# An interleaved two-model block on one core: new order inside the MLA and PLE stages, a stage boundary with a split moved between two adds, and 44 transposes after the second PLE

## The reference

```
ffn, even, ffn, ple, ffn, mla, ffn, ple, hybrid, ffn        then a final rms norm
ffn:    x = x + c * (silu(rms(x) @ gate) * (rms(x) @ up)) @ down       hidden width 2816
ple:    x = x + rms(sigmoid(rms(x) @ w_gate) * (p @ w_proj)) * gain
mla:    x = x + attention(8 heads, low-rank q and kv, rope) @ w_out
even:   a gated MLP over positions and a chunked recurrence; hybrid: attention, SSD and pooling
```

## Time and profile before

| | |
|---|---|
| median of 3 runs | 1418.93 us |
| the profiled execution, its own time | 1411.39 us |
| its span, first to last instruction | 1409.6 us |
| PE matmul busy | 96% of the span |
| DVE, ACT busy | 56%, 46% |
| mean granted TensorE clock | 0.981 |
| stages by time | FFN some 189 us each, even 140, MLA 108, hybrid 116, PLE 36 each |

### The profile page before, as it was taken

One profiled execution on the slowest core, in us unless ns is written; L12 is line 12 of the kernel. 1 busy time (PEld: TensorE's weight loads), 2 busy tenths in 40 slices (PEclk: granted clock), 3 DMA queues, 4 the chain that ended last, 5 costly groups with the idle time before them and its releaser, 6 DMA issues.

```text
span 1409.6 us, 17529 instructions
## 1 busy us (share of the span) xinstructions
PE 1346.7 (96%) x6634; PEld 1117.6 (79%) x6634; DVE 795.1 (56%) x860; ACT 644.2 (46%) x727; POOL 73.5 (5%) x180
## 2 busy tenths in 40 slices
PE   6999998999999999899999989999998998999997
PEld 5888888877888887688888867888886986788885
DVE  4555458635555556545446765644556796554543
ACT  5443456323544345543344754444345564543442
POOL 2000003000000000100000210000001200000000
PEclk9999999999999999899999999999999999999999
DMA  8555553413655555365554423655544451565550
GB/s 260 188 195 185 185 188 119 171 69 124 198 191 195 179 187 180 112 198 188 179 188 135 154 90 113 209 179 191 195 179 150 137 179 60 168 205 179 188 199 30
DMA packets 159116, 233.29 MB, mean 166 GB/s; under 512 B 7528, under 2 KB 126462, under 8 KB 159070
## 3 DMA queue, kind: packets, MB, share of 16 engines
q1 hardware_dynamic: 156420, 229.19, 48.8%
q10 hardware_dynamic: 2170, 2.68, 0.6%
q0 software_dynamic: 480, 0.80, 0.3%
HBM read 231.58 MB, written 1.05 MB: 165 GB/s over the span
## 4 chain that ended last, share of the span: by engine, by line
PE 86%; DVE 8%; ACT 4%; issue 1%; DMA 1%; POOL 0%; SPq 0%; ACTq 0%; POOLq 0%; DVEq 0%
PE ps L231 25%; PE ps L233 25%; PE ps L232 25%; DVE wl L203 3%; PE ps L470 2%; ACT wh L198 2%; PE ps L312 1%; PE ps L836 1%; PE ps L247 1%; DVE x_rows L412 1%; PE ps L249 1%; PE ps L248 1%; DMA raw<-in_ffn_w_up 1%; PE ps L1281 1%; ACT hth L332 1%
## 5 line engine op out<-in xcount | busy, mean ns | idle before, releaser
L231 PE MATMUL ps<-wl,hth 128*128 128x512 f32 (+2 forms) x1280 | 507.5, 396 | 18.7 <-DVE htl L345 9.4
L233 PE MATMUL ps<-wh,htl 128*128 128x512 f32 (+2 forms) x1280 | 497.9, 389 | 0.0
L232 PE MATMUL ps<-wh,hth 128*128 128x512 f32 (+2 forms) x1280 | 497.6, 389 | 0.0
L608 DVE TENSOR_TENSOR wl<-raw,wh 128x2048 fp32r<-128x2048 f32 x120 | 275.1, 2293 | 204.9 <-ACT wh L560 204.9
L231 PEld LDWEIGHTS ps<-wl,hth 128*128 128x128 f32 x1280 | 243.1, 190 | 70.9 <-issue 13.1
L203 DVE TENSOR_TENSOR wl<-raw,wh 128x2048 fp32r<-128x2048 f32 (+3 forms) x100 | 220.8, 2217 | 122.8 <-ACT wh L198 122.7
L560 ACT ACTIVATE wh<-raw 128x2048 fp32r<-128x2048 f32 x120 | 229.7, 1914 | 123.6 <-PE ps L233 123.6
L233 PEld LDWEIGHTS ps<-wh,htl 128*128 128x128 f32 x1280 | 242.6, 190 | 50.1
L232 PEld LDWEIGHTS ps<-wh,hth 128*128 128x128 f32 x1280 | 243.4, 190 | 45.9
L198 ACT ACTIVATE wh<-raw 128x2048 fp32r<-128x2048 f32 (+3 forms) x100 | 184.5, 1855 | 91.9 <-PE ps L233 70.3
L231 PE MATMUL ps<-wl,prod_h 128*128 128x512 f32 x400 | 156.1, 390 | 0.0
(11 more groups left out here) (351 smaller groups left out, 957.2 us busy)
## 6 DMA issues: line engine op xcount, KB each, us to landing
raw<-in_ffn_w_gate SPq DMA_DIRECT2D x88, 512.0 KB, 4.0
raw<-in_ffn_w_up SPq DMA_DIRECT2D x88, 512.0 KB, 4.9
raw<-in_ffn_w_down SPq DMA_DIRECT2D x88, 512.0 KB, 3.9
raw<-in_w_gate_up SPq DMA_DIRECT2D x44, 512.0 KB, 4.6
raw<-in_even_w_in SPq DMA_DIRECT2D x24, 512.0 KB, 4.6
raw<-in_w_down SPq DMA_DIRECT2D x22, 512.0 KB, 3.9
raw<-in_ple_w_gate SPq DMA_DIRECT2D x16, 512.0 KB, 3.7
raw<-in_w_in SPq DMA_DIRECT2D x16, 512.0 KB, 4.3
```

The costliest lines, as they stand in the source:

```text
L231: nc.tensor.matmul(o, xh, b, start=first, stop=False)
L232: nc.tensor.matmul(o, xh, a, start=False, stop=False)
L233: return nc.tensor.matmul(o, xl, a, start=False, stop=last)
L608: nc.vector.tensor_tensor(wl[:, r, :], raw[:, r, :], wh[:, r, :].bitcast(f32), ALU.subtract)\
```

## The change

Four parts. (1) `add_result`: only the next stage's first slot is split ahead of the adds, and the second between the halves. (2) PLE: gate slots n+1 and n+2 as before; then tile 0 with slots n+3 and n+4, then tile 1 with the same two, which stay in the ring until the end. The steps after it are done tile by tile, and `x_ready` counts four quarters. Where an FFN follows, its `x` is turned by tile and half (`turn_tile`), the first pieces stand inside the PLE's queues, and the FFN's first two slots are multiplied tile by tile. (3) Where none follows, TensorE makes 44 transposes of the identity into a free bank. (4) MLA: another order on ACT and DVE, one swap on PE, and a one-column exponential ahead.

The core of the diff:

```diff
         def add_result(dve, s, scale):
-            dve_ahead.before(dve, base[s] + SLOTS_OF[PLAN[s]] - 1)
+            following = base[s] + SLOTS_OF[PLAN[s]]
+            dve_ahead.through(dve, following)
             for half in range(2):
+                if half == 1:
+                    dve_ahead.through(dve, following + 1)
...
+            def first_by_tiles(pe):
+                turn_tile(pe, s, 0, 0)
+                turn_tile(pe, s, 0, 1)
+                for tt in range(TT):
+                    for u in range(2):
+                        take_slot(pe, n + u)
+                        turned_by(pe, s, 0, 2 * tt + u + 1)
+                        r = (n + u) % RING
+                        for kk in range(4):
+                            k, at = 4 * u + kk, kk * 2 * HC
+                            m = product(bank(tt), hth[:, k, tt * P:(tt + 1) * P], htl[:, k, tt * P:(tt + 1) * P],
+                                        wh[:, r, at:at + 2 * HC], wl[:, r, at:at + 2 * HC], k == 0, k == KT - 1)
+                            if tt == 0 and k == 5:
+                                turn_tile(pe, s, 1, 0)
+                                turn_tile(pe, s, 1, 1)
...
-            project_out(pe, s, 1, n + 1, by_halves=False)
...
+            for tt in range(TT):
+                for j in (2, 3):
+                    take_slot(pe, n + 1 + j)
+                    for kk in range(2):
+                        for half in range(2):
+                            m = gate_piece(j, kk, half, tt)
+                    if tt == 1:
+                        m.then_inc(weights_used, 1)
+                if tt == 0:
+                    m.then_inc(tile_ready, 1)
+            pe.wait_ge(ple_gate.sem, ple_gate.after("sigmoid0", l))
+            for _ in range(0 if after_ple(s + 1) else 44):
+                nc.tensor.transpose(ps[:, 4, 0:P], ident[:, :], ident[:, :])
...
+            gated(0)
+            gain(0)
+            add(0)
+            if after_ple(s + 1):
+                for u in range(2):
+                    tile_dve(dve, s + 1, 0, u, FFN_GAIN[fs[s + 1]])
+            gated(1)
+            if after_ple(s + 1):
+                dve_ahead.through(dve, n + 6)
+            gain(1)
+            add(1)
...
             act_ahead.through(act, n + 8)
+            q_rows(1)
             act.wait_ge(ML_ACT.sem, ML_ACT.after("v1"))
             act.wait_ge(ML_DVE.sem, ML_DVE.after("k1"))
...
-            q_rows(1)
             q_square(1)
...
             q_square(2)
+            nc.scalar.activation(m_exp, minus_half[:, 0:1], ACT.Exp)
             q_cols(1, 5)
             probs(0)
-            act_ahead.through(act, n + 10)
             q_rows(3)
+            probs(1)
             columns(0)
             k_cols(1, 4, 7)
-            probs(1)
-            q_square(3)
             q_cols(2, 6)
             q_cols(3, 4)
-            act_ahead.through(act, n + 11)
             columns(1)
             row_high(0)
             probs(2)
+            q_square(3)
...
+            dve_ahead.through(dve, n + 9)
             maxima(0)
+            k_scale(1)
             maxima(1)
             q_rope_cols(1, 6)
-            k_scale(1)
-            dve_ahead.through(dve, n + 9)
...
-            dve_ahead.through(dve, n + 10)
             row_low(0)
             maxima(3)
             rows(1)
-            dve_ahead.through(dve, n + 11)
-            for h in range(2, MH):
+            q_squares(3)
+            maxima(4)
+            row_low(1)
+            rows(2)
+            dve_ahead.through(dve, n + 10)
+            for h in range(3, MH):
...
```

More of the change, by code:

```diff
@@ L319, in turn_x @@
             else:
-                pe.wait_ge(x_ready, 4 * (s - 1) + 2 * (b // 2 + 1))
+                pe.wait_ge(x_ready, 4 * (s - 1) + (3 + b // 2 if PLAN[s - 1] == "ple" else 2 * (b // 2 + 1)))
             turn_bank(b, KT, x, to)
@@ L485, in chunk @@
                 turn_product()
[L488 to L502, removed]
+            if after_ple(s):
+                first_by_tiles(pe)
+            else:
+                first_by_features(pe)
             for half in range(2):
@@ L609, in split @@
                   .then_inc(split_ready, 1)
-            norm_dve(dve, s, FFN_GAIN[f], FFN_BANKS)
+            if after_ple(s):
+                for u in range(2):
+                    tile_dve(dve, s, 1, u, FFN_GAIN[f])
+            else:
+                norm_dve(dve, s, FFN_GAIN[f], FFN_BANKS)
             dve_ahead.through(dve, n + 3)
@@ L635, in build_block, with after_ple @@
         FFN_BANKS = (2, 3, 4, 6)
+        def after_ple(s):
+            return s > 0 and PLAN[s - 1:s + 1] == ["ple", "ffn"]
         last_h, last_l = hth[:, KT - 2:KT, :], htl[:, KT - 2:KT, :]
@@ L697, in ple_act, with sigmoid @@
             rms(act, s)
-            act_ahead.before(act, n + 4)
-            for tt in range(TT):
+            act_ahead.through(act, n + 5)
+            def sigmoid(tt):
                 if tt == 0:
@@ L706, in ple_act, with squares @@
                                                    scale=rstd[:, tt:tt + 1]), f"sigmoid{tt}", l)
-            for tt in range(TT):
+            def squares(tt):
                 act.wait_ge(ple_vector.sem, ple_vector.after(f"product{tt}", l))
@@ L710, in ple_act @@
                                                    accum_out=ple_ms[:, tt:tt + 1]), f"squares{tt}", l)
+            sigmoid(0)
+            squares(0)
+            act_ahead.through(act, n + 6)
+            if after_ple(s + 1):
+                for u in range(2):
+                    tile_act(act, s + 1, 0, u, FFN_GAIN[fs[s + 1]])
+            sigmoid(1)
+            squares(1)
+            if after_ple(s + 1):
+                nc.scalar.activation(xn[:, 0, :], x[:, 0, :], ACT.Square, scale=1 / math.sqrt(D),
+                                     accum_out=mean_sq[:, 0:1]).then_inc(sq_ready, 1)
+                act_ahead.through(act, n + 7)
         def ple_pool(pool, s, l):
```

124 lines of the change are left out of this document (95 added, 29 removed).

## The result

| | before | changed |
|---|---|---|
| first comparison, median of 4 and 4 runs | 1419.2 us | 1402.59 us (1396.58 to 1405.85) |
| the changed kernel once more (e12), 13 and 6 runs | 1410.83 us (1409.85 to 1413.45) | 1403.56 us (1398.35 to 1408.55) |
| profiled execution: time, span, mean granted clock | 1411.39, 1409.6, 0.981 | 1396.58, 1394.8, 0.991 |

The account below looks back on a forecast made before the run. TensorE, busy 96% of the span, was taken as the bound, so only its waits and half-clock stretches pay. Terms -3.0, -4.3, -7.4 and +2.1 sum to -12.6, from 1418.9 to 1406.3 us, range 1396 to 1417.

Parts of the forecast that it names:

- Second PLE: Between the second PLE and the hybrid: earlier turns of x and a clock held by 44 transposes, -3.0 us.
- The three parts of the forecast: After the second PLE: turns start 1.1 us earlier, turns take 0.8 less, ten products at full clock save 1.0.
- The rival, transposes at a fallen clock: After the second PLE: the 44 transposes don't hold the clock; term +0.9 to -1.1, total about 9.6, 1409 us; chance 0.2.
- First PLE: First PLE and the next FFN's first two slots: product starts 6.5 us earlier, later waits remain; -4.3 us.
- The lower value: FFN after the first PLE: if the clock falls again at 566.7, the gain is 3.8 us instead of 5.2.
- a sign of trouble: Listed under wrong: a POOL root that takes over 1 us behind DVE's split.
- MLA: MLA stage: waits removed 4.5 us, half clock behind them 3.2, less a new wait of 0.35; -7.4 us.
- (a): MLA: the 1.4 us wait for ACT's copy of q, behind the exponential's table load and a split, goes.
- (b): MLA: the 0.7 us wait for q goes, the copy now standing ahead of a square of 1.0 us.
- (d): MLA: the 0.7 us wait for divided rows is filled by scores(4), 2 us.
- Ends of stages: Stage ends: the second slot's split between the adds delays next products, 1.35 after MLA, 0.65 after the hybrid; +2.1 us.
- The sum: Whole kernel: -3.0 - 4.3 - 7.4 + 2.1 = -12.6 us, median 1418.9 to 1406.3 us; chance 0.45.

Follow-up runs that it names:

- e12: The changed kernel once more, unaltered, against the kernel before on the same chip; 1403.56 us against 1410.83, ratio 0.9955.
- e7: The changed kernel with 200 transposes instead of 44 between the second PLE and the hybrid; the 200 took 21.99 us, 0.11 each.
- e3: The changed kernel without the 44 transposes after the second PLE; 1403.53 us, ratio 0.9933 to the kernel before.
- e1: The changed kernel with the next stage's second slot split ahead of the four adds again, as before; 1396.3 us, ratio 0.9886 to the kernel before.
- e8: The changed kernel, second slot split between the adds only ahead of a PLE, elsewhere later, and the last gain row's DMA later; 1396.92 us, ratio 0.9872.
- e5: The kernel before with the MLA part of the change alone; 1405.72 us, ratio 0.9938, MLA stage 99.68 us.
- e9: The changed kernel with MLA slot n+10's two splits (ACT and DVE) back in their old places; 1406.31 us, ratio 0.995, MLA stage 103.33 us.
- e10: The changed kernel without the early one-column exponential on ACT in MLA; MLA stage 99.90 us, 1406.28 us in one execution.
- e4: The kernel before with only the second slot's split moved between the adds; 1418.34 us against 1412.92, ratio 1.003.

## Why the prediction was right, and where it was not

- *Second PLE, -3.0:* measured -3.09. The turns start 5.4 us after the end of the last matmul (5.7 forecast, 6.75 before). The three parts of the forecast, 1.1, 0.8 and 1.0, come to 2.9. The dispute was the clock in the 44 transposes, and e7 decides it. The rival, transposes at a fallen clock, gave this term +0.9 to -1.1. e3, which has no transposes, measured -1.90: its first product comes 1.30 us earlier than before, and its fall costs 2.1 us of busy time where that of before costs 2.7.
- *First PLE, -4.3 between 3.8 and 5.2:* measured -5.06, with the clock at 1.00. The lower value was wrong: I took the middle because a fall of the clock at the first product would cost 1.4 us of the end. In two later kernels (e1, e8) the clock did fall there, for 3.4 us, and the stage took 192.76 and 192.73 us all the same, with the table load of the first silu 19.23 us after the PLE's last matmul in both (19.27 at full clock). The stage got no longer because the wait of 1.29 us for the split was gone: TensorE at half clock reached the split only when it was done. The stretch in e1 (columns as in the earlier trace rows) and ACT's table load:

```profile
566.00:569.00 3.00, 3.00 (x9) 2.32 (x8) 3.00 (x3) 1.68 (x4) 0.41 (x1) 0.50 0.00 0
...
580.85 1.28 ACT L601 ACT_TABLE_LOAD   x1 [0.79 <-PE ps L233]
```

The POOL root did what I had named as a sign of trouble: 1.00 and 1.40 us for two operations on one column beside DVE's split and gain product, where the same two took 0.22 and 0.56 at 558.6. It cost little, since DVE had the gain product to do and waited 0.46 more.
- *MLA, -7.4:* measured -7.57 for the stage, of which the later first product takes back 0.19; e5 -7.87. Waits and clock went together as the forecast had it; e9 put one wait back and the clock fell behind it. Of its parts, (a) was argued from a table load and a split on ACT; e10 and e9 put each back, one at a time, and no wait came. The rows of e9 say that ACT has no slack left with the split alone, so that the two together make the 1.4 is likely; no run has both. Parts (b) and (d) were not tried alone either.
- *Ends of stages, +2.1 between 0 and 4.5:* this is the term that was mis-sized. The places were right (+1.36 after MLA, +0.68 after the hybrid, 0.36 back ahead of each PLE; 1.8 in all), but the time lost is 4.2 us in e4 by its ratio (1.6 to 7.1 by the interval), and some 6 between e1 and e3, on one chip and after the 1.2 of the transposes. I priced the gap and not the clock behind it: with first products 0.1 to 1.4 us later, the clock was at half behind 13 of 24 such starts (2 of 9 with the old adds), at 1.4 to 3.0 us of busy time each. I had written the gains of ending such falls into the sum, and not the cost of making new ones.
- *The sum:* -12.6, against -14.8 between the profiled executions (-12.4 without the start and the even stage) and -7.3 by the closer comparison. The profiled execution was the changed kernel's fastest of ten, with a clock of 0.991; its losses behind the ends of even, MLA and hybrid were 1.4 us; in e3 and e10, which have the same adds, 6.4 and 4.4. That difference is the mis-sized term again.
- The even stage was taken as unchanged but for its start. Its 1.25 us are no effect of the change: its clock losses were 9.6 us of busy time before and 6.6 in the changed kernel's first profile, and 16 in e8 and e10.

## What to carry to other kernels

Where TensorE bounds the kernel, price a gap ahead of a stage as its length plus the half clock that may follow, and count it against every edit that delays a first product, not only in favour of those that close a gap. If a wait stands behind the fall, it can take the loss up, as in e1 and e8 after the first PLE. When a wait cannot be removed, transposes of a unit matrix into an idle bank are a cheap cover if they end before the wait does, and are worth trying before a new order of the work: here 44 of them and an earlier add gave 3.9 of the 5.1 us. Transposes that outlast the wait cost their full time (e7: the turns start 16.3 us later). Judge such edits by stage lengths and clocks in the profile, since whole executions of one kernel spread by 12 us.

## What the runs showed of the hardware

- With full-width float32 transposes alone the granted clock stayed at 1.00 for 22 us (e7). Behind 4 us in which TensorE was 100% busy, mostly or wholly with some 50 to 90 products of 128x8, it fell in all 14 profiles, at 261.3 to 264.5 us.
- One fall lasted 20.5 us, 18.7 of them busy (e8, 307.5 to 328.0; e10 alike), in code that the changed kernel's first profile ran at 1.00. These two profiles are the only ones in which no fall began at 299 to 303, a few us ahead. What decides between the two stays open.
- POOL's operations on one column took 1.00 and 2.31 us beside a split of 2.28 on DVE (the second at 574.1) and 1.40 beside the gain product, and 0.22 and 0.56 with DVE idle. The timeline of POOL in the changed kernel:

```profile
558.56 0.22 POOL L823 TENSOR_SCALAR arena<-arena 128x1 f32<-128x1 f32 x1 [15.94 <-ACT arena L803]
558.86 0.56 POOL L824 TENSOR_TENSOR arena<-arena,minus_half 128x1 f32<-128x1 f32 x1
566.77 1.00 POOL L823 TENSOR_SCALAR arena<-arena 128x1 f32<-128x1 f32 x1 [7.35 <-ACT arena L803]
567.86 1.40 POOL L824 TENSOR_TENSOR arena<-arena,minus_half 128x1 f32<-128x1 f32 x1
```
